# Zero-padded per-head scaled queries in the chunked mLSTM of a hybrid encoder kernel

## The reference, cut to what matters

```
w = exp(dmat - m_t) * einsum('bhtd,bhsd->bhts', qc, kc)
s_inter = exp(m_inter - m_t)
num = s_inter * einsum('bhtd,bhdv->bhtv', qc, C) + einsum('bhts,bhsv->bhtv', w, vc)
den = s_inter * einsum('bhtd,bhd->bht', qc, n) + w.sum(axis=-1)
h = num / maximum(abs(den), exp(-m_t))
C_new = decay * C + einsum('bhs,bhsd,bhsv->bhdv', wk, kc, vc)
```

## Time and profile before

| what | value |
|---|---|
| median of the runs | 1757.62 us |
| the profiled execution's own time | 1759.72 us |
| its span in the trace | 1758.0 us |
| granted TensorE clock, mean | 0.975 |
| PE busy | 1644.4 us, 94% |
| PEld busy | 776.7 us |
| DVE busy | 600.6 us |
| ACT busy | 196.8 us |
| POOL busy | 280.2 us |

### The profile page before, as it was taken

One profiled execution on the slowest core, in us unless ns is written; L12 is line 12 of the kernel. 1 busy time (PEld: TensorE's weight loads), 2 busy tenths in 40 slices (PEclk: granted clock), 3 DMA queues, 4 the chain that ended last, 5 costly groups with the idle time before them and its releaser, 6 DMA issues.

```text
span 1758.0 us, 32322 instructions
## 1 busy us (share of the span) xinstructions
PE 1644.4 (94%) x13825; PEld 776.7 (44%) x13825; DVE 600.6 (34%) x1060; ACT 196.8 (11%) x415; POOL 280.2 (16%) x354
## 2 busy tenths in 40 slices
PE   7999999999999999899989898998989998989976
PEld 5666675554554445433433333343333333433324
DVE  5554445554451013561313113132222221312225
ACT  2211011221220001100000000000000000000001
POOL 1120121000005001312121211112112121121101
PEclk9999999999999999899999999999999999999999
DMA  7441433111115224499999999999999999999996
GB/s 254 138 127 53 150 104 84 47 39 51 36 36 165 79 75 188 174 381 412 423 421 430 421 423 424 388 426 427 426 397 418 427 424 416 416 422 427 423 427 277
DMA packets 95595, 495.64 MB, mean 282 GB/s; under 512 B 11504, under 2 KB 62944, under 8 KB 77632
## 3 DMA queue, kind: packets, MB, share of 16 engines
q1 hardware_dynamic: 81936, 460.58, 64.8%
q0 software_dynamic: 13040, 32.61, 5.4%
q10 hardware_dynamic: 496, 0.56, 0.1%
HBM read 475.07 MB, written 23.89 MB: 284 GB/s over the span
## 4 chain that ended last, share of the span: by engine, by line
PE 74%; DMA 23%; issue 2%; DVE 1%; SPq 0%; ACT 0%; POOL 0%; POOLq 0%; ACTq 0%; DVEq 0%
PE PS L2038 26%; PE PS L480 22%; DMA ring<-in_w 20%; PE PS L2050 7%; PE PS L1859 6%; PE PS L1947 3%; PE PS L1902 2%; PE PS L1820 2%; DMA ring<-y_dram 1%; PE PS L1906 1%; PE PS L1892 1%; PE PS L1704 1%; DMA x_sb<-in_x 1%; PE PS L2123 0%; PE PS L1680 0%
## 5 line engine op out<-in xcount | busy, mean ns | idle before, releaser
L2038 PE MATMUL PS<-ring,mix_sb 128*32 128x512 f32 x5376 | 611.6, 613 | 61.8 <-DMA ring<-in_w 60.7
L2038 PEld LDWEIGHTS PS<-ring,mix_sb 128*32 128x32 f32 x5376 | 173.4, 113 | 482.3 <-issue 393.3
L2050 PE MATMUL PS<-ring,hm_sb 128*32 128x256 f32 x5376 | 296.3, 379 | 0.9 <-DMA ring<-in_w 0.7
L1586 DVE TENSOR_TENSOR low_sb<-PS,low_sb 128x1536 f32<-128x1536 f32 (+1 forms) x32 | 49.9, 1558 | 606.2 <-PE PS L2038 606.2
L2050 PEld LDWEIGHTS PS<-ring,hm_sb 128*32 128x32 f32 x5376 | 172.2, 110 | 132.5 <-issue 19.0
L480 PE MATMUL PS<-uT_sb,ring 128*128 128x512 f32 (+2 forms) x368 | 134.2, 521 | 0.0
L839 POOL COPY ints<-ints 128x3 int32 (+1 forms) x30 | 5.6, 186 | 674.4 <-ACT hm_sb L1046 674.4
L1040 ACT ACTIVATE hm_sb<-hm_sb 128x768 f32<-128x768 f32 (+1 forms) x32 | 24.5, 766 | 709.8 <-DVE hm_sb L1588 709.8
L784 POOL DMA_INDIRECT mix_sb<-xt_dram,ints x84 | 86.3, 1028 | 64.7 <-POOL ints L826 23.0
L480 PEld LDWEIGHTS PS<-uT_sb,ring 128*128 128x128 f32 x368 | 69.3, 190 | 60.2 <-issue 56.2
L480 PE MATMUL PS<-ring 128*128 128x129 f32 (+4 forms) x328 | 88.1, 393 | 0.0
(11 more groups left out here) (337 smaller groups left out, 1285.6 us busy)
## 6 DMA issues: line engine op xcount, KB each, us to landing
ring<-in_w SPq DMA_DIRECT2D x58, 4096.0 KB, 20.2
ring<-in_w SPq DMA_DIRECT2D x72, 2048.0 KB, 20.5
ring<-in_w_in SPq DMA_DIRECT2D x24, 512.0 KB, 4.4
ring<-in_w_in SPq DMA_DIRECT2D x8, 1024.0 KB, 5.3
y_dram<-at_sb POOLq DMA_DIRECT2D x4, 2048.0 KB, 10.9
ring<-in_w SPq DMA_DIRECT2D x8, 1024.0 KB, 5.1
ring<-y_dram SPq DMA_DIRECT2D x4, 2048.0 KB, 23.4
ring<-m_dram POOLq DMA_DIRECT2D x16, 256.0 KB, 4.6
```

Of the source, the lines that this page charges most:

```text
L1586: V.tensor_tensor(hid, PS[:, at:at + g, :], b1_row.unsqueeze(1).broadcast_to([P, g, 2 * QR]), ALU.add).then_inc(hid_used, 1)
L2038: last = nc.tensor.matmul(PS[32 * j:32 * j + 32, at + t, :].rearrange("p (c n) -> p c n", c=2), xgT[n][:, k, 32 * t:32 * t + 32], w1_c[k][ ...
L2050: last = nc.tensor.matmul(PS[32 * j:32 * j + 32, Y_BANK + t, 0:QR], actT[:, k, 32 * t:32 * t + 32], w2_in[k // 2][:, k % 2, j * QR:(j + 1) ...
```

## The change

`q_in`, one tile for both heads with head 0's rows above head 1's, becomes two tiles, one for each head, moved to slot 7. In the tile of head hh the other head's 64 rows are zero. They are zeroed once, by GpSimd, ahead of the loop over pairs; as slot 7 is read by DVE until `low_used` is 3, GpSimd waits for that first. For each pair GpSimd now makes `q_in` in four products of 64 partitions, where there were two of 128. The PV matmuls against a state take all 128 rows of the padded `q_in` and of the state, so the other head's state is multiplied by zeros. TensorE waits for `q_in` once a head. GpSimd has one wait more for its own products.

```diff
-    q_fall, q_in = view(ring, slot(4), 2, T), view(ring, slot(4) + 2 * T, 2, T)
+    q_fall = view(ring, slot(4), 2, T)
+    q_in = [view(ring, slot(7) + 2 * T * hh, 2, T) for hh in range(2)]
...
         pool.wait_ge(rows_stored, 32)
+        pool.wait_ge(low_used, 3)
+        for hh in range(2):
+            other = DQK * (1 - hh)
+            nc.gpsimd.memset(q_in[hh][other:other + DQK], 0.0).then_inc(q_in_ready, 1)
+        pool.wait_ge(q_in_ready, 2)
...
-            for d in range(2):
-                nc.gpsimd.tensor_tensor(q_in[:, d, :], qT, q_fall[:, d, :], ALU.mult).then_inc(q_in_ready, 1)
+            for hh in range(2):
+                h = slice(DQK * hh, DQK * hh + DQK)
+                for d in range(2):
+                    nc.gpsimd.tensor_tensor(q_in[hh][h, d, :], qT[h, :], q_fall[h, d, :], ALU.mult).then_inc(q_in_ready, 1)
+            pool.wait_ge(q_in_ready, i * 4 + 6)
+            passed(pool)
...
-            pe.wait_ge(q_in_ready, i * 2 + 2)
             pe.wait_ge(s_used, i * 3 + 3)
             for hh in range(2):
                 if hh == 1:
                     pe.wait_ge(oexp_ready, i * 2 + 2)
-                h = slice(DQK * hh, DQK * hh + DQK)
+                pe.wait_ge(q_in_ready, i * 4 + (2 * hh + 4))
                 for m in range(MT):
                     c = slice(m * P, (m + 1) * P)
-                    fwd = [(q_in[h, 0, c], state_f[m][h]), (diagonal(hh, 0)[:, c], v_sb[:, m, hh, :])]
+                    fwd = [(q_in[hh][:, 0, c], state_f[m]), (diagonal(hh, 0)[:, c], v_sb[:, m, hh, :])]
                     bwd = [(diagonal(hh, 1)[:, c], v_sb[:, m, hh, :])]
                     if m < MT - 1:
-                        bwd = [(q_in[h, 1, c], state_b[m][h])] + bwd
+                        bwd = [(q_in[hh][:, 1, c], state_b[m])] + bwd
```

## The result

The changed kernel took 1747.55 us, the median of five runs (1744.49 to 1750.02), against 1757.62 us (1756.23 to 1758.46). The ratio is 0.9943, 95% interval 0.9931 to 0.9955: 10.1 us faster, between 7.9 and 12.1. Forecast were 1746.5 us and a range of 1742.0 to 1752.0. The profiled execution has a span of 1745.8 us.

The account below looks back on a forecast made before the run. PE itself was taken as the path through the mLSTM, 48.2 us of it in PV. -21.6 + 1.0 + 7.4 + 2.1 = -11.1 us took the median from 1757.62 to 1746.5 us, range 1742.0 to 1752.0.

Parts of the forecast that it names:

- Part 1: PV blocks: 60 records of one height at 0.112 us, 6.7 instead of 12.05 us; saves 21.6 us over four pairs.
- Part 2: After each PV block PE waits 0.25 us for DVE's reading of head 0; +1.0 us, bounds 0 and 2.0.
- Rival 2: PV: state products, not height changes, set the pace; padded records stay at 0.201 us; 1767.1 us, chance 0.05.
- Rival 3: PV: same-row weight loads don't run beside matmuls; 0.300 us a record, blocks of 18.0 us; 1790.9 us, chance 0.01.
- Part 3: Pair 0: row loads queue behind GpSimd's low_used wait and memsets; PE waits 7.4 us at the meta-token value product.
- Part 4: Behind pair 0's PE wait the clock runs at half speed for a stretch; +2.1 us, kept within 1.4 and 2.7.
- Rival 4: Clock stays low for long after pair 0's wait, costing 6.7 to 8.5 us; 1752.0 us, chance 0.06.
- What was put at nothing: GpSimd's longer q_in products and its wait for them, and the clearing store 13 us later: no cost.
- Rival 1: Pair 0's wait costs nothing: key copies still beat PE's need or loads aren't held up; 1737.0 us, chance 0.04.

Follow-up runs that it names:

- Experiment 3: Kernel before, unpadded, PV products reordered per head: forward state products, v products of both directions, backward state products; six height changes a pair, not 28; 1737.98 us.
- Experiment 6: Kernel before, unpadded, PV reordered so both heads' 64-row forward state products alternate and head 0 finishes ahead of head 1; 1739.31 us, ratio 0.9895.
- experiment 1: Changed kernel with the low_used wait and the zeroing moved behind pair 0's row loads; 1736.88 us, ratio to the kernel before 0.9878.
- experiment 2: Kernel before plus only the low_used wait and two memsets of 64x1024 ahead of the row loads, no padded products; 1768.06 us, ratio 1.0055.
- experiment 7: Kernel before plus only the low_used wait ahead of the row loads, no memsets; 1765.18 us, ratio 1.0048.
- experiment 4: The changed kernel run again without an edit, on the same chip as other follow-ups; 1746.84 us, ratio to the kernel before 0.9931.
- experiment 5: Changed kernel with the two zeroings moved to DVE behind low_used, GpSimd having neither wait nor memsets; 1735.95 us, ratio to the kernel before 0.9878.

## Why the prediction was right, point by point

- **PV in one form** (Part 1): 60 records at 0.112 us were put at 6.7 us a block. Measured are 6.79 with what there is of Part 2's wait in it. Experiment 3 shows the cause apart from the pad, and its 7.33 us block fits the same price of 0.19 us a change. Rivals 2 and 3 had been set aside on three records alone; the block of 60 bears that out. In the groups of the changed kernel, 106.1 to 112.9 us, loads of 192 ns lie beside matmuls:

```profile
L481 PE MATMUL PS<-ring 128*128 128x129 f32 x60 | 6.9, 275 | 0.0
L481 PEld LDWEIGHTS PS<-ring 128*128 128x128 f32 x59 | 6.7, 192 | 0.2 <-issue 0.2
```

  Rival 3's block of 18.0 us isn't there. The Trainium skill ("TensorE: Matmul & The Clock Gate", Part 3, The mechanism) says in one sentence that loads overlap matmuls only if the row groups differ, and in another that a load into the background weight buffer runs ahead too. This trace goes with the second and against the first: loads of 192 ns on the same rows ran beside matmuls that follow each other every 113 ns.
- **Head 0 wanted sooner** (Part 2): 0.25 us a pair, bounds 0 and 0.5. It was smaller: PE went on 0.11 us behind DVE's end, not 0.2 to 0.3, so that less than 0.1 us of wait is left in a block (112.96 against 112.89). The starts of PV are (268.14 - 106.17) / 3 = 53.99 us apart, 54.1 by the forecast. The net saving, from PV of pair 0 to the end of PV of pair 3, is 20.99 us, against 21.6 - 1.0 = 20.6 by the sum. Experiment 6 shows the wait in the open.
- **The row loads behind the wait** (Part 3): first load at 70.6 expected, 69.72 measured, with an opening 1.0 us earlier (67.8 and 1.9 make 69.7 and not the 69.9 of the text; the 0.2 that it doesn't name was there, 66.74 to 66.93, and the two memsets of 64 partitions took 1.95); PE to go on at 86.1, measured 85.14 and 85.43; rows landed 10.2 us behind the first load's issue, 10.0 expected. The wait itself was given as 7.4 us with bounds of 6.4 and 8.8 and came out at 9.08 in one profile, outside them, and 6.66 in another, since it is the rest up to a date. The step of the sum that should have been worded otherwise is this one: the date is the term, not the wait.
- **The clock** (Part 4): 2.1 us expected within 1.4 and 2.7, 2.6 and 2.8 measured in the two profiles of the changed kernel (2.7 and 2.9 against the 18.33 of experiment 1), 2.75 and 2.1 in experiments 2 and 7. For the changed kernel the term was too small by 0.5 to 0.8. The slow stretch went from 80.6 to 90.7, of which 5.6 us were work; behind the longer of the two waits of the earlier trace rows it was 5.5, and I had taken a middle between that and 3.4. Rival 4, a clock that stays low for long after the wait, didn't come: from 90.8 to the end of PV of pair 3 it is 1.00.
- **Parts 3 and 4 together** were 9.5 us. Experiment 2 gives 10.3, and the difference between experiments 4 and 1 gives 10.0. The sum came out at -11.1, measured -10.1 in the first group and -10.9 in the second. That it fits so closely is in part luck: in the profile of experiment 4 the wait was 0.7 us shorter and the slow clock 0.7 us dearer than forecast, and the two misses cancel.
- **What was put at nothing** cost nothing that the profile shows: GpSimd's 5.1 us of products had 17 us of cover in pair 0, its clearing store went out 12 us later and PE had no new wait up to the attention, and the gain went through attention and mixing undiminished.
- **Rival 1**, that pair 0 pays nothing, was priced at 1737.0. It isn't what the change does, but it is what the pad does once the row loads go first: 1736.88.

## What to carry to other kernels

Look at the distance between starts of records, not at their durations: a stream that alternates between operands of 64 and 128 rows ran at 0.208 us a record here, and records of either height ran at 0.112 when like stood beside like. Either padding or a new order brings that, and the order needs no extra buffer. Where a one-time set-up stands in a queue, look at what is issued behind it: here two memsets and a wait ahead of the first row loads took back half of the gain, and the same set-up behind the loads, or on an engine with cover, cost nothing.

## What the runs showed of the hardware that I had not expected

- Going from one 64-row half of the array to the other costs no pause: in experiment 3 the two heads' 64-row records meet inside the 14 records that take 1.42 us with their change of height, 0.34 us less than 14 x 0.112 + 0.19. In experiment 6, which was to use this, 22 records of 64 rows, 16 of them of both heads in alternation, take 98.33 - 96.57 = 1.76 us; one after the other they would take 22 x 0.112 + 0.19 = 2.65. Records on the two halves ran at the same time. The kernel before shows the same, and the prediction didn't use it: its scores are 64-row matmuls of both heads in alternation, and 16 of them take 88.36 - 87.27 = 1.09 us, 0.068 us a record with a change of height in front.

```profile
87.27 1.16 PE L1760 MATMUL PS<-ring 64*128 64x128 f32 x16
88.36 1.76 PE L1773 MATMUL PS<-ring 128*64 128x129 f32 x28
```

- A wait of 9 us was followed by 5.5 us of work at half clock, one of 4.7 us (experiment 7) still cost 2.1 us. A short stretch at 0.50 near 64 us, inside the value projection, came in some executions and not in others: the projection took 14.05 us in the first profile of the changed kernel and 15.74 in the second, of the same program. Experiments 1 and 5 have 14.05, the kernel before and experiments 2, 3, 6 and 7 have 15.74. With one profile each, how often it comes isn't known, and why it comes is not shown; a difference of 1.7 us between two single profiles can be this alone.
